# Two sets of 32x32 products at a time between projection steps in the chunked solve of a fused four-layer model

## The reference

```python
def rwkv7_step(state, inp):
    r_t, w_t, k_t, v_t, kk_t, a_t = inp
    sa = jnp.einsum('bhvk,bhk->bhv', state, -kk_t)
    state = (state * w_t[:, :, None, :]
             + sa[..., None] * (kk_t * a_t)[:, :, None, :]
             + v_t[..., None] * k_t[:, :, None, :])
    y = jnp.einsum('bhvk,bhk->bhv', state, r_t)
    return state, y
...
z = h @ even_w_in[j]
a_val, a_glu, a_gate, r, k, v, wd, ad, b_gate = split_cols(z, EVEN_SIZES)
ya = conformer_conv(a_val, a_glu, conv_w[j], conv_vec[j]) * jax.nn.silu(a_gate)
yb = rwkv7_mix(r, k, v, wd, ad, rwkv_mu_rkv[j], rwkv_mu_lora[j], rwkv_vec[j], ...)
out = jnp.concatenate([ya, yb * jax.nn.silu(b_gate)], axis=-1) @ even_w_out[j]
x = x + gate[:, None, :] * out
```

## Time and profile before

| | us |
|---|---|
| median of 3 runs | 1766.77 (1765.31 to 1768.53) |
| the profiled execution, its own time | 1764.11 |
| its span in the trace | 1762.4 |
| TensorE busy | 1664.6 (94%) |
| VectorE busy | 1235.5 (70%) |
| the eight pairs of the first layer | about 80 to 634 in the span |

### The profile page before, as it was taken

The page is one execution under the profiler, slowest core; times in us unless marked ns, Lnnn a source line. Parts: engine busy times, 40 slices in busy tenths (PEclk is TensorE's granted clock), DMA queues, the critical chain, the costliest instruction groups (busy, mean ns, idle before and its releaser), DMA issues.

```text
span 1762.4 us, 38758 instructions
## 1 busy us (share of the span) xinstructions
PE 1664.6 (94%) x16172; PEld 1267.4 (72%) x16172; DVE 1235.5 (70%) x2231; ACT 806.0 (46%) x1505; POOL 795.9 (45%) x713
## 2 busy tenths in 40 slices
PE   5899999999989899999999999999999999999997
PEld 5677776777776668757777777787777778777766
DVE  7578878988879788269997777535887436355553
ACT  3544444454443273365544444434767433444443
POOL 3534334344342245457883222544545545544433
PEclk9999999999999999999999999999999999999998
DMA  7212311312313123212221111123222232433312
GB/s 305 95 63 74 110 54 70 121 51 74 121 51 133 38 96 125 96 48 73 84 96 49 37 37 37 61 96 108 72 84 71 82 99 81 140 115 117 109 57 90
DMA packets 51902, 155.12 MB, mean 88 GB/s; under 512 B 5888, under 2 KB 12032, under 8 KB 51600
## 3 DMA queue, kind: packets, MB, share of 16 engines
q1 hardware_dynamic: 51728, 152.65, 25.6%
HBM read 150.50 MB, written 2.13 MB: 87 GB/s over the span
## 4 chain that ended last, share of the span: by engine, by line
PE 66%; DVE 20%; ACT 5%; issue 4%; POOL 2%; DVEq 0%; POOLq 0%; ACTq 0%
PE bank L524 16%; PE bank L528 14%; PE bank L525 14%; PE bank L1272 7%; PE bank L2360 3%; DVE ya L1599 2%; DVE best L2468 2%; DVE lru_xc L2852 2%; DVE score L2471 2%; PE bank L3077 1%; PE bank L1230 1%; PE bank L2390 1%; PE bank L3092 1%; DVE probs_t L2515 1%; PE bank L570 1%
## 5 line engine op out<-in xcount | busy, mean ns | idle before, releaser
L498 POOL TENSOR_TENSOR w_lo<-raw,w_hi 128x512 fp32r<-128x512 f32 (+2 forms) x434 | 578.6, 1349 | 603.2 <-ACT w_hi L480 591.7
L524 PE MATMUL bank<-h_hi,w_hi 128*128 128x512 f32 x1368 | 578.1, 423 | 10.2 <-ACT h_hi L973 2.5
L528 PE MATMUL bank<-h_lo,w_hi 128*128 128x512 f32 x1368 | 543.3, 397 | 10.8 <-DVE h_lo L941 6.3
L525 PE MATMUL bank<-h_hi,w_lo 128*128 128x512 f32 x1368 | 541.5, 396 | 0.0
L480 ACT ACTIVATE w_hi<-raw 128x512 fp32r<-128x512 f32 (+2 forms) x434 | 248.1, 603 | 252.7 <-PE bank L528 172.0
L524 PEld LDWEIGHTS bank<-h_hi,w_hi 128*128 128x128 f32 x1368 | 260.9, 191 | 100.2 <-issue 34.0
L528 PEld LDWEIGHTS bank<-h_lo,w_hi 128*128 128x128 f32 x1368 | 260.7, 191 | 77.1 <-DVE h_lo L941 11.4
L525 PEld LDWEIGHTS bank<-h_hi,w_lo 128*128 128x128 f32 x1368 | 261.5, 191 | 57.4 <-issue 9.3
L1599 DVE SCALAR_TENSOR_TENSOR ya<-padded,vecs,ya 128x512 f32<-128x512 f32 x240 | 214.2, 893 | 3.9
L3153 DVE CUSTOM_DVE_ANT_0 fox_probs<-bank,fox_keybias 128x128 f32<-128x128 f32 (+3 forms) x64 | 28.9, 488 | 84.7 <-PE bank L3077 84.4
L524 PE MATMUL bank<-own_hi,w_hi 128*128 128x512 f32 x208 | 82.9, 398 | 1.6 <-ACT own_hi L973 1.6
(11 more groups left out here) (412 smaller groups left out, 2826.8 us busy)
## 6 DMA issues: line engine op xcount, KB each, us to landing
raw<-even_in SPq DMA_DIRECT2D x57, 512.0 KB, 3.7
raw<-odd_in SPq DMA_DIRECT2D x39, 512.0 KB, 3.2
raw<-ada SPq DMA_DIRECT2D x32, 512.0 KB, 4.0
raw<-fox_in SPq DMA_DIRECT2D x25, 512.0 KB, 3.3
raw<-lru_in SPq DMA_DIRECT2D x24, 512.0 KB, 3.2
ada_first<-ada SPq DMA_DIRECT2D x16, 512.0 KB, 13.7
raw<-even_out SPq DMA_DIRECT2D x16, 512.0 KB, 3.3
raw<-odd_out SPq DMA_DIRECT2D x16, 512.0 KB, 3.3
```

Of the source, the lines that this page charges most:

```text
L498: e.tensor_tensor(k.w_lo[s % NSPLIT][:, at], k.raw[n % NRAW][:, at], k.w_hi[s % NSPLIT][:, at].bitcast(F32), ALU.subtract).then_inc(*did(" ...
L524: e.matmul(out, hi[:, w], x[i][0], start=start and i == 0, stop=False, skip_group_check=True)
L525: e.matmul(out, lo[:, w], x[i][0], start=False, stop=False, skip_group_check=True)
L528: m = e.matmul(out, hi[:, w], x[i][1], start=False, stop=stop and i == kt - 1, skip_group_check=True)
```

## The change

Nothing is computed otherwise, and no instruction is added or taken away. In all three tables the sets of 32x32 products are moved among the projection steps. Before, `sq2 sq2p sq3 sq3p` stood in a row behind `tB`; now `r0` stands ahead of them, `r1 r2` between `sq2p` and `sq3`, and `r3 r4` between `sq3p` and `sq4`. After `sq4` only one step (`r5`) stands before `off0`, where there were three, and one (`r6`) before `merge0`, where there were two. `merge1` comes one step earlier. The other engines' tables follow: VectorE gets its taps elsewhere, `ada0` goes from behind `sq4` to behind `turn1`, and `ada1` from behind `merge0` and one tap to behind `merge1` and one tap; ScalarE takes `wk0` and `wk1` later, GpSimd `below` earlier.

```diff
 ORDER = {
     "tensor": """
...
-        gate7' k7 Z sq1 tK tB sq2 sq2p sq3 sq3p r0 r1 sq4 r2 r3 r4 off0 r5 r6 merge0 kk_sum r7 off1 v0 v1
-        v2 v3 merge1 v4 v5 v6 v7 PAt U0 PA G C glu0 glu1 chain1 glu2 chain2 glu3 chain3 glu4 glu5 glu6 glu7 chain4
+        gate7' k7 Z sq1 tK tB r0 sq2 sq2p r1 r2 sq3 sq3p r3 r4 sq4 r5 off0 r6 merge0 kk_sum r7 off1 v0 v1
+        v2 merge1 v3 v4 v5 v6 v7 PAt U0 PA G C glu0 glu1 chain1 glu2 chain2 glu3 chain3 glu4 glu5 glu6 glu7 chain4
...
     "vector": """
...
-        sq1 tap3 tB tap4 sq2 sq2p k_lerp sq3p f_out tap5 sq4 ada0 tap6 turn0 tap7 tap8 merge0 tap9 ada1 turn1 tap10
-        tap11 tap12 tap13 tap14 tap15 merge1 tap16 PAt tap17 G tap18 C tap19 chain1 chain2 ada2 chain3 kk_norm tap20
+        sq1 tap3 tB tap4 sq2 tap5 sq2p k_lerp tap6 sq3p f_out tap7 sq4 turn0 tap8 tap9 merge0 turn1 ada0 tap10 tap11
+        tap12 merge1 tap13 ada1 tap14 tap15 tap16 PAt tap17 G tap18 C tap19 chain1 chain2 ada2 chain3 kk_norm tap20
...
     "scalar": """
-        tA wval0' wval1' decay f_square f_log f_root powers wgate0' wgate1' before rate gate_done' N sq1 Z wk0 k_copy wk1 sq2
-        tK sq3 off0 kk_sq off1 kk_root r_copy wr0 wr1 wv0 v_copy U0 PA wv1 wglu0 V glu_done t1 wglu1""",
+        tA wval0' wval1' decay f_square f_log f_root powers wgate0' wgate1' before rate gate_done' N sq1 Z k_copy sq2 wk0
+        tK sq3 wk1 off0 kk_sq off1 kk_root r_copy wr0 wr1 wv0 v_copy U0 PA wv1 wglu0 V glu_done t1 wglu1""",
     "gpsimd": """
-        prior wgate0' inner wgate1' k_diff wk0 below wk1 r_diff wr0 wr1 wv0 wv1 v_diff wglu0 wglu1 wval0
+        prior wgate0' inner wgate1' k_diff below wk0 wk1 r_diff wr0 wr1 wv0 wv1 v_diff wglu0 wglu1 wval0
...
 LAST_ORDER = {
     "tensor": """
...
-        gate7' gate0 gate1 gate2 gate3 gate4 gate5 gate6 gate7 cg00 sq2 sq2p sq3 sq3p mean2 mean3 mean4 mean5 mean6
+        gate7' gate0 gate1 gate2 gate3 sq2 sq2p gate4 gate5 sq3 sq3p gate6 gate7 cg00 mean2 mean3 mean4 mean5 mean6
```

More of the change, by code:

```diff
@@ L1103 @@
         glu5 glu6 glu7 val0 val1 val2 val3 val4 val5 val6 val7 tA^ mm0^ bonus_sum tV^ k0^ w_up^ k1^ k2^ k3^ k4^ k5^
-        mm1^ N^ k6^ k7^ Z^ sq1^ tK^ tB^ sq2^ sq2p^ sq3^ sq3p^ r0^ r1^ sq4^ r2^ r3^ r4^ off0^ r5^ r6^ merge0^
-        kk_sum^ r7^ off1^ v0^ v1^ v2^ v3^ merge1^ v4^ v5^ v6^ v7^ PAt^ U0^ PA^ G^ C^ glu0^ glu1^ chain1^ glu2^
+        mm1^ N^ k6^ k7^ Z^ sq1^ tK^ tB^ r0^ sq2^ sq2p^ r1^ r2^ sq3^ sq3p^ r3^ r4^ sq4^ r5^ off0^ r6^ merge0^
+        kk_sum^ r7^ off1^ v0^ v1^ v2^ merge1^ v3^ v4^ v5^ v6^ v7^ PAt^ U0^ PA^ G^ C^ glu0^ glu1^ chain1^ glu2^
         chain2^ glu3^ chain3^ glu4^ glu5^ glu6^ glu7^ chain4^ val0^ val1^ chain5^ val2^ val3^ val4^ val5^ val6^
@@ L1109 @@
         cum powers carry k_lerp kk_norm A B r_lerp R rk v_lerp V mm0^ val_done tV^ tap0^ cum^ powers^ mm1^ N^ N_t^
-        carry^ tap1^ tap2^ sq1^ tap3^ tB^ tap4^ sq2^ sq2p^ k_lerp^ sq3p^ tap5^ sq4^ ada0^ tap6^ turn0^ tap7^ tap8^
-        merge0^ tap9^ ada1^ turn1^ tap10^ tap11^ tap12^ tap13^ tap14^ tap15^ merge1^ tap16^ PAt^ tap17^ G^ tap18^ C^
+        carry^ tap1^ tap2^ sq1^ tap3^ tB^ tap4^ sq2^ tap5^ sq2p^ k_lerp^ tap6^ sq3p^ tap7^ sq4^ turn0^ tap8^ tap9^
+        merge0^ turn1^ ada0^ tap10^ tap11^ tap12^ merge1^ tap13^ ada1^ tap14^ tap15^ tap16^ PAt^ tap17^ G^ tap18^ C^
         tap19^ chain1^ chain2^ ada2^ chain3^ kk_norm^ tap20^ ada3^ chain4^ A^ chain5^ B^ r_lerp^ chain6^ R^ U^ rk^
@@ L1115 @@
         decay wk0 powers before rate k_copy kk_sq wk1 wr0 kk_root r_copy v_copy wr1 wv0 wv1 wglu0 V glu_done wglu1 tA^
-        wval0 wval1 decay^ powers^ before^ rate^ N^ sq1^ Z^ wk0^ k_copy^ wk1^ sq2^ tK^ sq3^ off0^ kk_sq^ off1^ kk_root^
+        wval0 wval1 decay^ powers^ before^ rate^ N^ sq1^ Z^ k_copy^ sq2^ wk0^ tK^ sq3^ wk1^ off0^ kk_sq^ off1^ kk_root^
         r_copy^ wr0^ wr1^ wv0^ v_copy^ U0^ PA^ wv1^ wglu0^ V^ glu_done^ t1^ wglu1^""",
     "gpsimd": """
-        prior wk0 k_diff wk1 wr0 wr1 wv0 wv1 wglu0 r_diff v_diff wglu1 wval0 wval1 prior^ inner^ k_diff^ wk0^
-        below^ wk1^ r_diff^ wr0^ wr1^ wv0^ wv1^ v_diff^ wglu0^ wglu1^ wval0^ wval1^"""}
+        prior wk0 k_diff wk1 wr0 wr1 wv0 wv1 wglu0 r_diff v_diff wglu1 wval0 wval1 prior^ inner^ k_diff^ below^
+        wk0^ wk1^ r_diff^ wr0^ wr1^ wv0^ wv1^ v_diff^ wglu0^ wglu1^ wval0^ wval1^"""}
 ORDER = {
@@ L1156 @@
     "scalar": """
-        tA f_square f_log f_root wval0' wval1' N sq1 wgate0' Z tK wgate1' gate_done' gate_done sq2 sq3 off0 wgate0 wgate1
+        tA f_square f_log f_root wval0' wval1' N sq1 wgate0' Z tK wgate1' gate_done' sq2 sq3 gate_done off0 wgate0 wgate1
         wcg00 off1 cg_done0 wcg01 wcg10 wcg11 U0 PA cg_done1 cg_done2 centre0 centre1 t1 f_square^ centre2 centre3 centre4
```

## The result

The changed kernel takes 1778.19 us in the median (1772.73 to 1783.08, 8 runs), the kernel before 1766.92 (1764.35 to 1768.53, 8 runs): the ratio is 1.0067, with a 95% interval of 1.0053 to 1.0081. It is slower by 11.3 us, where 1773.5 and "slower" had been forecast. The profiled execution took 1777.44, 13.3 more than that of before.

A forecast was written before the change was run, and what follows sets the result against it. TensorE, busy 94% of the span, was taken as the bound. The terms -16 + 17.9 - 1 + 2 + 4 = +6.9 on 1764.1 gave 1771.0, plus 2.7 for the median, said as 1773.5 us; 8-in-10 range 1760 to 1784.

The forecast's parts named there:

- Part 1, the gain: Stretch from sq1 to merge0, pairs 0 to 6: spreading the sets takes 96.8 us against 112.84, a gain of 16.
- What the blocks are: TensorE's "issue" gaps: fetches of 256 instructions, each started only when a block is used up, 3.65 us where binding.
- Part 2, the wait: Before C: later ada1 delays the loads of glu and val, so C waits 2.55 us in seven pairs, 17.9 us.
- Part 3, given back: At f_sum2: VectorE catches up while TensorE is later at C, so 1 us comes back (0 to 3.3).
- Part 4, pair 7: Last pair: TensorE idles 3.7 us before sq2, most of the wait before sq3 is filled; about 2 us more.
- Part 5, the clock: Around C: the new idle brings the half clock in three of seven pairs at 1.3 us, 4 us (0 to 9).
- The gain stands: Rival, chance 0.13: U0 does not wait for the loads, or they land early enough; sum -15, 1752 us.
- The fetch is hidden: Rival, chance 0.15: from sq1 to merge0 only the wait for VectorE was real; gain 22, sum +1, 1768 us.
- Clearly slower: Rival, chance 0.14: half clock from the idle before C in all seven pairs, fetches 4.2 us a block; +21, 1788 us.

The follow-up runs named there:

- e5: The kernel before with 128 more TensorE instructions (32x32 products) ahead of the first pair: 1770.1 us, ratio 1.0031.
- e10: The kernel before with 512 more 32x32 products over the four array quarters in turn, ahead of the first pair: 1794.4 us, ratio 1.0161.
- e1: The changed kernel with VectorE's ada1 directly behind ada0, ahead of merge1, and merge1 one tap earlier, in pairs 0 to 6: 1756.3 us, ratio 0.9949.
- e2: The kernel before with only VectorE's ada0 moved behind turn1 and ada1 behind merge1 and one tap: 1798.3 us, ratio 1.0185.
- e4: The changed kernel with v_copy, U0 and PA ahead of wr0 wr1 wv0 in ScalarE's queue: 1766.9 us, ratio 1.0012.
- e3_last_undone: The changed kernel with the table of the last pair (7) put back to that of before: 1774.1 us, ratio 1.0047.
- e11: The changed kernel with 128 more TensorE instructions ahead of the first pair: 1781.8 us, ratio 1.0088.
- e6: e1 with the table of the last pair (7) put back to that of the kernel before: 1754.2 us, ratio 0.9938.
- e9: The kernel before with 512 more 32x32 products in one corner of the array, ahead of the first pair: 1818.9 us, ratio 1.0306.
- e8_ada0_early: e6 with VectorE's ada0 one place earlier, behind turn0, and ada1 directly behind turn1: 1754.0 us, ratio 0.9939.

## Why the prediction was right, step by step

**Part 1, the gain: right in its sum, partly by luck in its pieces.** 16.3 against 16. The price of a block, 3.65, was measured as 3.73. But the working's 96.8 was for the starts of `merge0`, and these sum to 92.3. What comes 16.3 us earlier is its end, by VectorE's sum, since in pairs 0 and 4 (and, shorter, in 1) a stop falls inside `merge0`. The long pairs were to be 0, 1, 4 and 5; they are 0, 4 and 6. The new stop of 0.4 before `r0` did not come, as its premise was wrong: `k_copy` runs from 1.56 to 2.16 after `sq1`, near the forecast's 2.2, but `r0` starts at 1.53 in all seven pairs, straight behind `tB`, and so does not need the bank that it empties. And the gain did not come where it was worked out: the stops for instructions gave 1.1 us, the wait for VectorE 6.3, and the half clock, assumed gone and not priced, the busy time's 8.7, half the gain.

**What the blocks are: right, with two corrections.** The stops are fetches of 256 instructions, as e5, e10 and the packets show. Matmuls and loads alone, 32,344, left the count 2 short of the 128 packets; with the 555 records of TensorE's sequencer it is 32,899, or 128.5 times 256. And a fetch does not wait until a block has been used up: in e10 it begins 1.05 to 1.63 us into a block that has 1.93 us of work.

**What the sum lacked.** From the sum of `merge0` to `PAt` 4.1 us came on: in pairs 0 and 4 the half clock behind the stop inside `merge0` (1.4 us each), in pairs 2 and 3 a stop for instructions behind it (0.52 and 0.66 us idle, the stretches 0.8 and 0.9 longer). The working ended at `merge0`, as though the blocks did too.

**Part 2, the wait: right, each link.** 18.6 against 17.9 us. From the sum of `merge0` to the loads' issue 7.55 had been worked out (8.35 less 0.8); in pair 5 it is 7.57, in pair 4, with its stop and half clock, 8.99. Link by link: copy to issue 2.26 (2.25), issue to `wr0` 3.81 (3.8). e1, e2 and e4 show by three ways that it is this chain: shortened it gives 22 us (3.8 of them ahead of `PAt`), put into the kernel before it costs 33, passed by in ScalarE's queue it gives 11. The four other moves (`ada0`, `wk0`, `wk1`, `below`) were not undone by themselves; TensorE's wait for `w_lo` is 1.1 us before and after.

**Part 3, given back: wrong.** `f_sum2` waits 3.2 us as before (3.3), not 1 less. That VectorE comes later by what TensorE does would explain it, but no run tests that.

**Part 4, pair 7: right.** 1.7 against 2, and the idle is there, 3.5 us for the 3.7 forecast. TensorE's last step before `sq2`, and `sq2`:
```profile
575.94 0.39 PE L528 MATMUL bank<-h_lo,w_hi 128*128 128x512 f32 x1
579.81 0.38 PE L1272 MATMUL bank<-W 32*32 32x32 f32 x23 [3.48 <-DVE W L1647]
```
e3_last_undone found 4 us in the time of the whole; by the traces pair 7 is 3.1 us shorter in it.

**Part 5, the clock: right in kind, low in size.** Five pairs of seven have the half clock behind `C`, not three, and 6.6 us were lost from `C` to the next `sq1`, not 4. The stretch behind `C` in pair 4, which has it, the one around the wait before (`C` starts at 402.19, the clock falls at 403.0), and the one before `C` in pair 5, which has not:
```profile
402.90:406.40 3.50, 3.50 (x34) 2.35 (x26) 2.45 (x3) 0.30 (x1) 2.55 (x3) 0.52 0.00 0
399.60:403.00 3.40, 1.25 (x75) 1.11 (x73) 2.19 (x4) 3.34 (x8) 2.97 (x3) 1.00 0.03 8
466.00:469.40 3.40, 1.17 (x62) 0.89 (x54) 2.88 (x5) 2.85 (x6) 2.28 (x2) 1.00 0.20 78
```
TensorE was busy 1.25 us of 3.4 where the clock fell and 1.17 where it did not. These stretches were cut by eye and do not settle what decides. Over the runs, waits of 2.4 us before `C` were followed by the half clock in 5 of 7 pairs (in e11 in 7), the idle of some 3 us in e2 in 6 of 7, the waits of up to 1.8 us of e1, e4 and e6 in none. Why the same wait is followed by it in one pair and not in another stays open, and the three pairs of seven in the forecast were a guess.

**The rivals.** "The gain stands" would have been right without `ada1`: e1_ada1_early is that case, 1756.3 against 1752. "The fetch is hidden" falls with e5 and e10. It had one thing right: the idle that went was mostly the wait for VectorE (6.3 of 7.6 us). The Trainium skill, "Runtime: NRT & Kernel Launch", section "Instruction fetch mechanics", calls crossing a block mostly hidden. Here it is hidden in e9 (6.8 us of work in a block) and not in e10 (1.93 us of work, 3.73 in all), so the measurements bound the rule. "Clearly slower" had the half clock in all seven pairs and blocks of 4.2 us; it was five pairs and 3.73.

The forecast's sum of +6.9 met +13.3 in the profiled execution: 4.1 of the difference is what came behind `merge0`, 2.6 the clock, 1 `f_sum2`, 0.7 the wait at `C`, and the rest, about -2, has the other sign.

The version to keep is e8_ada0_early, or e6_both: TensorE's new order with `ada1` ahead of `merge1` and the last table as it was. Both are 0.6% faster than the kernel before, where the change as made is 0.7% slower.

## What to carry to other kernels

When sets of tiny matmuls stand in a row, count instructions, not only busy time: here 256 of them in a row cost 3.7 us where their own work was 1.9, and 256 with 6.8 us of work met no stop. Wide work put between them fills a part of the stop. When tables for several engines are rewritten together, follow each moved step to the DMA that its end sets free, and from there through every in-order queue to the engine that sets the time; the step that cost most (`ada1`) was on an engine busy 70% of the span. And follow a stop past the end of the stretch in question, since it can come back behind it.

## What the runs showed that was not expected

- Four loads of 512 KB whose buffers come free together go out within 1.7 us, and the third lands 7.0 us after its issue (pair 5 of e1_ada1_early), where the first of two takes 3.7 to 3.9 (the changed kernel): moved early, `ada1` was early by less than it seemed.
- 32x32 products in one corner of the array: TensorE counts as busy for all of 53 us and was granted 0.50 throughout, 53 ns a matmul. Over the four quarters 128 matmuls take 1.93 us at the same clock, 15 ns each. Though busy for all of the 53 us, TensorE did not get the full clock there.
- The first stop in e10's row is 4.53 us long, the six behind it 1.53 to 2.08. The packet that ends it starts at 52.38, 11.0 us after the one before it; why so late, no run shows.
